# A differential attention layer with its projection slabs woven into the head steps, and a state-space scan that takes its heads in pairs

## What is computed

```python
def diff_pool_layer(x, ...):                       # stage A
    proj = rms_norm(x, norm_g) @ w_in              # 1024 -> q 512, k 512, v 512, u 512
    q, k, v, u = jnp.split(proj, ...)
    q, k = rms_norm per 64-wide half head          # 4 heads, 2 halves each
    a_out = diff_attention(q, k, v, lam, ...)      # softmax(q0 k0) - lam * softmax(q1 k1), times v, causal, ALiBi,
                                                   # then rms_norm over the 128 columns of a head
    b_out = pool_mixer(u, w_group, pool_scale)     # trailing mean minus token, 4 groups of 128, a 128x128 map each
    return x + concat([a_out, b_out]) @ w_out      # 1024 -> 1024

scores = cb[...] * decay                           # scan S: per head and chunk of 128 tokens
y_diag = einsum('bcgels,bcsgep->bclgep', scores, xdt)
y_off  = einsum('bclgn,bcgepn->bclgep', cm, states_in) * exp(a_cs)
```

## Time and profile before

| | |
|---|---|
| median of 3 runs | 2020.97 us (2020.79 to 2022.02) |
| the profiled execution | 2023.49 us, its span 2021.3 us |
| mean granted TensorE clock | 0.984 |
| PE busy | 1944.0 us, 96% of the span |
| DVE, ACT, POOL busy | 1180.1, 795.6, 130.5 us |
| chain that ended last | PE 84%, DVE 9%, ACT 4% |
| moved by DMA | 186.49 MB, mean 92 GB/s |

### The profile page before, as it was taken

How to read it: one execution, slowest core, us unless ns; L and a number is a source line. 1 busy time by engine, 2 the same in 40 slices (tenths; PEclk the granted TensorE clock), 3 DMA queues, 4 the chain that set the end, 5 groups by cost and what they waited for, 6 DMA issues and landing times.

```text
span 2021.3 us, 24744 instructions
## 1 busy us (share of the span) xinstructions
PE 1944.0 (96%) x9034; PEld 1529.7 (76%) x9034; DVE 1180.1 (58%) x1847; ACT 795.6 (39%) x1231; POOL 130.5 (6%) x104
## 2 busy tenths in 40 slices
PE   7967999999999999999999999999999999999999
PEld 6834788888877667888887877777766678888877
DVE  3377566526644765765367487554465657653672
ACT  3144443313433654442234333322356644422341
POOL 2020100000011101000000100111111010000000
PEclk9977999999999999999999999999999999999999
DMA  5200232232222111222221323234342212222213
GB/s 203 94 11 1 83 104 98 79 114 85 79 96 84 63 42 63 85 97 94 99 104 62 115 84 117 99 130 152 120 151 94 79 63 84 98 94 99 104 60 106
DMA packets 38016, 186.49 MB, mean 92 GB/s; under 512 B 4353, under 2 KB 4481, under 8 KB 23089
## 3 DMA queue, kind: packets, MB, share of 16 engines
q1 hardware_dynamic: 37648, 185.22, 26.5%
q10 hardware_dynamic: 288, 0.23, 0.0%
HBM read 176.95 MB, written 8.49 MB: 92 GB/s over the span
## 4 chain that ended last, share of the span: by engine, by line
PE 84%; DVE 9%; ACT 4%; issue 2%; DMA 0%; POOL 0%; SPq 0%; DVEq 0%; ACTq 0%; POOLq 0%
PE banks L676 58%; PE banks L1100 15%; DVE w_lo L1777 1%; DVE tmp L2160 1%; PE banks L1039 1%; PE banks L1017 1%; PE banks L925 1%; PE banks L1026 1%; DVE w_lo L2027 1%; PE banks L1141 1%; PE banks L989 1%; PE banks L1166 1%; ACT w_hi L1265 1%; PE banks L1113 1%; ACT w_hi L1459 1%
## 5 line engine op out<-in xcount | busy, mean ns | idle before, releaser
L676 PE MATMUL banks<-xn_hi,w_hi 128*128 128x512 f32 x1288 | 506.3, 393 | 17.9 <-DVE w_lo L2520 9.6
L676 PE MATMUL banks<-xn_hi,w_lo 128*128 128x512 f32 x1288 | 503.3, 391 | 0.0
L676 PE MATMUL banks<-xn_lo,w_hi 128*128 128x512 f32 x1288 | 498.1, 391 | 0.0
L1777 DVE TENSOR_TENSOR w_lo<-raw,w_hi 128x2048 fp32r<-128x2048 f32 (+2 forms) x139 | 287.2, 2066 | 79.5 <-ACT w_hi L1265 79.4
L1265 ACT ACTIVATE w_hi<-raw 128x2048 fp32r<-128x2048 f32 (+2 forms) x139 | 237.6, 1709 | 225.2 <-PE banks L676 225.2
L676 PEld LDWEIGHTS banks<-xn_hi,w_hi 128*128 128x128 f32 x1288 | 243.2, 189 | 73.0 <-issue 19.9
L676 PEld LDWEIGHTS banks<-xn_lo,w_hi 128*128 128x128 f32 x1288 | 243.1, 189 | 51.7 <-issue 1.0
L676 PEld LDWEIGHTS banks<-xn_hi,w_lo 128*128 128x128 f32 x1288 | 243.3, 189 | 50.8
L1343 ACT ACTIVATE tmp<-scaled_h,par 128x512 f32<-128x512 f32 x132 | 100.6, 809 | 349.7 <-DVE scaled_h L1860 349.7
L676 PE MATMUL banks<-hid_hi,w_hi 128*128 128x512 f32 x528 | 206.4, 391 | 6.9 <-DVE w_lo L1777 5.1
L676 PE MATMUL banks<-hid_lo,w_hi 128*128 128x512 f32 x528 | 205.8, 390 | 0.0
(11 more groups left out here) (258 smaller groups left out, 2387.2 us busy)
## 6 DMA issues: line engine op xcount, KB each, us to landing
raw<-weights SPq DMA_DIRECT2D x116, 1024.0 KB, 4.8
raw<-weights SPq DMA_DIRECT2D x24, 768.0 KB, 4.2
raw<-weights SPq DMA_DIRECT2D x24, 640.0 KB, 3.8
big<-scratch SPq DMA_DIRECT2D x40, 256.0 KB, 4.9
att<-scratch SPq DMA_DIRECT2D x16, 256.0 KB, 4.2
scratch<-stage SPq DMA_DIRECT2D x12, 256.0 KB, 4.2
scratch<-con SPq DMA_DIRECT2D x12, 256.0 KB, 2.2
x<-xt SPq DMA_DIRECT2D x4, 512.0 KB, 8.3
```

Of the source, the lines that this page charges most:

```text
L676: return pe.matmul(psum[:, 2 * p + m, :], w[:, at_:at_ + P], x_part(k), start=start, stop=stop)
L1777: dve.tensor_tensor(w_lo[:, sl], raw[:, sl], w_hi[:, sl].bitcast(F32), ALU.subtract).then_inc(lo_done, 1)
```

## The change

1. Slabs are reordered in stage A: the weights of q, k, v for heads 0 and 1 and of u come first (5 plain slabs, `A_IN`), then q, k, v for heads 2 and 3 (`A_MORE`, 3 slabs), then `A_OUT` in half slabs of 4 input chunks by 4 output chunks, first the two of the pooling half, then the two of the attention half.
2. `A_MORE` and the first two slabs of `A_OUT` are woven into 18 steps g, one for each (head, query block) and two at the end; the other two of `A_OUT` follow. Units use banks 2 and 3.
3. The norms, v transposes, pooling groups and their products, and the norm of each finished head (square, sum, scale, split) are spread over the slabs and the steps. POOL squares q, k and heads 0 to 2 and does three of the splits; it no longer copies v. The pooled chunks get their high part straight from PSUM on ACT, the low part on DVE.
4. The scan does both heads of a pair in one step, with the halves m in turn. `seg` and `c_grow` have 4 buffers each. A chunk of memory, `more` (3 x 512 columns), is added.
5. The first slab of `F0_U0` waits for units only if they used its banks.

```diff
-    ("A_IN", 8, 8, 2), ("A_OUT", 4, 8, 2),
+    ("A_IN", 5, 8, 2), ("A_MORE", 3, 8, 2), ("A_OUT", 4, 4, 4),
-WOVEN = ("C_K", ...)
+WOVEN = ("A_MORE", "A_OUT", "C_K", ...)
+A_FILL = weave([("A_MORE", 3), ("A_OUT", 2)], [20] * 4 + [16] + [12] * 4 + [7] * 8 + [8] + [12, 20])
+        more = at("more", 3 * T)

 PE, stage A
-                    linear("A_IN", xh, xl, (t_hi, xn_ready, 0), 0)
-                    attention("A", A_HEADS, 0, {"v": 0, "t": 0, "o": 0})
...
-                    linear("A_OUT", ...)
+                slab(0, 0, 8, 2, xh, xl, (t_hi, xn_ready, 0))
+                slab(1, 0, 8, 2, xh, xl, between=lambda: stat(0))
+                slab(2, 0, 8, 2, xh, xl, between=lambda: norm_job(0, 4))
+                norm_job(1, 5)
+                slab(3, 0, 8, 2, xh, xl, between=lambda: turn_v(0))
+                slab(4, 0, 8, 2, xh, xl)
+                pe.wait_ge(banks_read, 4)
+                for g in range(A_STEPS + 2):
+                    it = g // 4
+                    if g < A_STEPS:
+                        scores(g)
+                    fill(g)
+                    if 1 <= g <= A_STEPS:
+                        turn(g - 1)
+                    if g % 4 < 2 and it + 1 < A_HEADS:
+                        norm_job(2 * (it + 1) + g % 4, 1)
+                    elif g % 4 >= 2 and it < 2:
+                        pool_product(2 * it + g % 4 - 2)
+                    if g == 1:
+                        turn_v(1)
+                    elif g in (9, 10):
+                        turn_v(g - 7)
+                    elif g % 4 == 3 and it:
+                        squares_summed(it - 1)
+                    if g >= 2:
+                        values(g - 2)
+                fill(A_STEPS + 2)
+                squares_summed(A_HEADS - 1)
+                fill(A_STEPS + 3)
+                for s in (FIRST["A_OUT"] + 2, FIRST["A_OUT"] + 3):
+                    woven(s, 0, 48, a_sub_hi, a_sub_lo, sub_ready)

 DVE, stage A, a step g
+                    if 1 <= g <= A_STEPS:
+                        finish(g - 1)
+                    if g < A_STEPS:
+                        maxima(g)
+                    if g < 2:
+                        pool_group(2 + g)
+                    if g % 4 == 2 and it:
+                        output(it - 1)
+                    if g % 4 in (1, 2) and it + 1 < A_HEADS:
+                        scaled(2 * (it + 1) + g % 4 - 1)
+                    elif g in (3, 4, 7, 8):
+                        pooled_low(2 * ((g - 3) // 4) + (g - 3) % 4)
+                    if g % 4 == 0 and it >= 2:
+                        sub_scale(it - 2, chunk(big, it - 2))
+                    if g:
+                        for s, m in A_FILL[2][g - 1]:
+                            evacuate(s, m)
+                    for q in range(2):
+                        if g >= q + 1:
+                            for s in A_FILL[1][g - q - 1]:
+                                lo_piece(s + 1, q, 2)

 PE, scan (every second head's first step)
-                def head_products(h):
...
+                def pair_products(q):
...
+                    pe.wait_ge(score_ready, 2 * q + 2)
                     for j in range(4):
+                        for m in range(2):
+                            h = 2 * q + m
+                            pe.matmul(psum[64 * m:64 * m + 64, bank, j * P:(j + 1) * P], xdt[:, j, h * 64:h * 64 + 64],
+                                      seg[h % 4][:, j * P:(j + 1) * P], ...)
                     pe.wait_ge(st_taken, 3 * g + 3)
+                    pe.wait_ge(c_ready, 2 * q + 2)
                     for j in range(1, 4):
+                        for m in range(2):
+                            ...  state[j - 1], c_grow[h % 4]

 PE, slab()
-                    if woven_slab(s - 1) or woven_slab(s - 2):
+                    if (woven_slab(s - 1) or woven_slab(s - 2)) and unit_banks(UNITS_BEFORE[s] - 1) == 2 * p:
```

More of the change, by code:

```diff
@@ L220, in blocks_program @@
         bias = [chunk(att, 6), chunk(att, 7)]
[L221 to L227, removed]
+        sq_q, sq_k, sq_o = chunk(tn, 0), chunk(tn, 1), chunk(tn, 2)
+        sub_rs = chunk(more, 0)
         neg_max, row_sum, row_inv = small[:, 0:8], small[:, 8:16], small[:, 16:24]
@@ L325, in blocks_program @@
         acs = [chunk(att, 0), chunk(att, 1)]
-        seg = [chunk(att, 2), chunk(att, 3), chunk(tn, 2)]
+        seg = [chunk(att, 2), chunk(att, 3), chunk(tn, 2), chunk(more, 0)]
         grow = [rs, rsk]
-        c_grow = [chunk(tn, 0), chunk(tn, 1)]
+        c_grow = [chunk(tn, 0), chunk(tn, 1), chunk(more, 1), chunk(more, 2)]
         cs_t = tok[:, 0:192].rearrange("p (j h) -> p j h", j=4)
@@ L440, in body @@
                 def body(i):
-                    if not (a == 0 and isinstance(i, int)):
-                        slab(a, i, k * m * P)
+                    slab(a, i, k * m * P)
                     slab(a + 1, i, k * m * P)
[L444 to L447, removed]
                 if n:
-                    pairs(sp, n, body, head=1 if a == 0 else 0)
+                    pairs(sp, n, body)
                 if (hi - lo) % 2:
@@ L458, in _ @@
                 if step == "A":
-                    stream("A_IN")
-                    stream("A_OUT")
+                    slab(1, 0, slab_columns(1, 0))
+                    sp.dma_start(par[:, GAINS_AT:LATE_AT], params[:, GAINS_AT:LATE_AT]).then_inc(params_in, 16)
+                    late_loads()
+                    for s in range(2, FIRST["F0_U0"]):
+                        slab(s, 0, slab_columns(s, 0))
                 elif step == "C":
@@ L559, in _ @@
                     ffn(step)
-            last = 56
+            last = 48
             for q in range(4):
@@ L569, in _ @@
         def _(pool):
[L570 to L596, removed]
             def sum_squares(base):
@@ L1312, in rms @@
                 act.activation(to, lt[:, :], ACT.Exp, scale=-0.5).then_inc(ready, 1)
-            def high_parts(base, n, dst, c0=0):
-                for c in range(n):
-                    act.wait_ge(t_ready, base + c - DC + 1)
-                    act.activation(chunk(dst, c0 + c), chunk(tn, (base + c) % 3), ACT.Identity).then_inc(t_hi, 1)
             token_norms = [0]
@@ L1572, in decay @@
                     act.wait_ge(seg_ready, 4 * h + 4)
[L1573 removed]
+                    act.activation(seg[h % 4], seg[h % 4], ACT.Exp).then_inc(decay_ready, 1)
                 def square(c):
@@ L2589, in halves @@
     def halves(w):
-        for k in range(0, D, 512):
+        for k in range(0, w.shape[0], 512):
             for n in range(0, D, 512):
@@ L2602, in ffn @@
             c += half
-    linear(a["ab_w_in"][0])
-    linear(a["ab_w_out"][0])
+    for c in (0, 512, 1024, 1536, 1792, 256, 768, 1280):
+        linear(a["ab_w_in"][0], c, c + 256)
+    halves(a["ab_w_out"][0][512:])
+    halves(a["ab_w_out"][0][:512])
     ffn(a["f_w_up"][0], a["f_w_down"][0])
```

858 lines of the change are left out of this document (400 added, 458 removed).

## The result

| | before | changed |
|---|---|---|
| time, median (us) | 2021.27 (4 runs) | 1965.81 (4 runs, 1965.11 to 1966.84) |
| ratio | | 0.9723 [0.971, 0.9736] |
| profiled execution: span (us) | 2021.3 | 1965.1 |
| its mean granted clock | 0.984 | 0.997 |

A forecast was written before the change was run, and what follows sets the result against it. PE, busy 96% of the span, was taken as the bound, with idle time to fill in stage A and only PE's own work to shrink in the scan. 43.3 + 13.3 = 56.6 off 2020.97 gave 1964.4 us, range 1956 to 1976.

The forecast's parts named there:

- stage A: Whole of stage A: F0 starts at 200.4 instead of 243.7, saving 43.3 us.
- The scan: Scan: pairs of 28 records with column halves in turn save 12.4 us, fewer returns 0.9, together 13.3.
- The first five slabs: Start of stage A: five plain slabs with norm sums and v transposes, so the steps begin at 74.8.
- PE's own list: Stage A: PE's work at full clock without waits, 99.7 us for the steps, 21.9 for slabs 10 and 11.
- Wait (a): Stage A, step 2: PE waits 2.1 us for the second half of slab 6's low part from DVE.
- I take 1.00: Stage A's steps: granted clock stays full, since attention X weaves slabs into similar steps at 1.00.
- Wait (b): Stage A, step 15: slab 9 wants a bank that DVE reads behind its maxima, 0.5 us.
- Wait (c): Stage A's tail of half-slab pairs: X's first wait, 1.35 us, comes here too; its second, 1.02, does not.
- Rival 1: Stage A, steps 9 to 16: chain maxima, exponentials, finish sets the step, 36.1 us instead of 31.2; 1969.3 us; chance 0.17.
- Rival 2: Stage A, early steps: DVE-bound, POOL's squares meet low parts four times, 4 us more, 1968.4 us; chance 0.11.
- Rival 3: Scan: the column halves don't overlap, 12.4 us less is saved, 1976.8 us; chance 0.06.
- Rival 5: Stage A's steps: waits bring the clock to 1.2 GHz, up to 2064 us, slower from 57% of steps; chance 0.02.

The follow-up runs named there:

- n4: Changed kernel with DVE adding stage A's last output slab's first unit to x ahead of the low part of F0's first slab: 1964.98 us.
- n9: n8 with DVE's pooled low part ahead of step 7's maxima and slab 9's low pieces moved from steps 10 and 11 to ends of 12 and 13: 1956.88 us.
- n3: Changed kernel with slab 6's second high piece earlier on ACT and both its low pieces at the end of DVE's step 1: 1962.81 us.
- n7: n3 with DVE also reading slab 5's first unit out of its bank at the end of step 1: 1961.13 us.
- n2: Changed kernel with one head's 14 scan records in every second step, buffers and other engines' orders kept: 1981.77 us.
- n6: Changed kernel with 9 instead of 7 woven products in each of steps 9 to 16, and 6 and 10 instead of 12 and 20 behind: 1970.32 us.
- n1: Changed kernel with the pair's heads not in turn in the scan: products grouped by head as 4, 4, 3, 3: 1969.62 us.
- n5: Changed kernel with all seven scan products of a pair's first head, then all seven of the second: 1975.06 us.
- n8: n7 with n4's order of the tail in all three woven stages, A, C and X: 1956.76 us.
- n10: The changed kernel once more, with no edit: 1965.39 us.

## Why the prediction was right, and where it was off

The mechanism of both parts was as forecast. That the total came within 1.4 us (by the profiled spans within 0.4, 1965.1 against 1964.7) is luck in part, because errors had opposite signs: stage A gave 4.0 less than its term, the scan 2.6 more, and 1.0 in the stages between, nearly all of it clock, was in no term. Step by step:

- **The first five slabs**: the steps begin at 74.2, forecast 74.8.
- **PE's own list** (99.7 for the steps, 21.9 for slabs 10 and 11, 121.6): 204.43 - 74.24 = 130.2, less 8.1 of waits and 1.9 lost behind the first of them, is 120.2, where 1.9 holds 1.6 of clock and the 0.3 beyond the wait's length. That is 1.4 less than forecast; 1.0 of it are the 14 fp32 sums, most of which take 0.86 us where woven, not 0.93. The other waits have such extras too (taking away 1.36 in n4 gave 1.7, and 1.09, 0.97 and 0.50 in n9 gave 1.22, 1.19 and 0.72), so PE's own work is some 0.9 us less still.
- **Wait (a)**, slab 6's low part: forecast 2.1, it was 2.98. (The terms in that sum give 92.45 and not 92.6, so 2.0.) Place and cause were right (n3, n7). The step that failed is the sentence on the clock, "I take 1.00": true of 117 of the 130 us, but the clock came down behind the wait and cost 1.6 us more (it came down in six traces of seven that had the wait). X could not show that, since the earlier trace rows hold no wait of this size. The start of stage C in the trace of before could: behind a wait of 2.25 us there, products stand 0.43 apart and the granted clock of 16 us is 0.89.

```profile
622.42 0.47 PE L1100 MATMUL banks<-xn_hi,w_hi 128*128 128x512 f32 x1 [2.25 <-DVE big L2038]
```

- **Wait (b)**: forecast 0.5, it was 0.70. **Wait (c)**: forecast 1.35, it was 1.36, and the one after it stayed away, as forecast from the banks.
- **Waits not on the list**: 1.09 in step 7, 0.97 and 0.50 in steps 11 and 12, 0.49 behind the steps, 3.1 us together. The forecast had added up DVE's load per step and found room. n9 shows that load wasn't the matter: the order was, since a low-part piece (for which DVE itself waited on ACT) or the maxima stood ahead of what PE wanted. In all, 4.1 us of waits more than forecast and 1.9 behind the first of them, 1.4 and 0.6 less of work: the 4.0 that stage A lacks.
- **The scan**: 28 records of a pair took 1.68, forecast 1.79 from X's 16 records (8 x 0.11 = 0.9 us). A return to the fill costs 0.2 us and not 0.11, because the gap ahead of a head is wider too (n2); that and the shorter pair make 8 x 1.91 = 15.3 where 13.3 was forecast. The other 0.6 is a wait of the kernel before that had no term (n2).
- **Rival 1** (steps 9 to 16 bound by the chain) fell: they took 32.7 us with 2.2 of waits in them, 30.5 without, by the list 31.2; n6 lengthened them by the products it added. **Rival 2** fell: no piece of a low part in the early steps was slowed by POOL (1.21 to 1.22 us a piece, for half of what takes 2.29 in the earlier trace rows). What it describes came once and late: slab 10's two pieces took 3.45 us at 170.31 beside POOL. PE's 0.49 us behind the steps come after that on DVE; that they follow from it was not tested. **Rival 3**: n1, n5 and n2 gave back 3.8, 9.3 and 16.0 us; the halves do overlap. **Rival 5**, the slow side, was there in small: 0.87 over 13.4 us, which is some 3.5 us at the low clock and not 57% of the steps.

On rival 3, what X's rows had said holds in the scan as well: all 14 products of a pair use the same 128 rows, and their records run two at a time. The Trainium skill (TensorE: Matmul & The Clock Gate, Part 3: Packing small matmuls) says that a weight load overlaps matmuls in flight only when its row group differs. By that rule n2 and the changed kernel would have differed only by the returns, 1.9 us; they differ by 16.0, so the measurement decides against it here. The same section of the Trainium skill also gives a speedup of 2.38 for three products packed by columns. The prediction left that out, and the runs bear it out in kind: two column halves share the time.

That TensorE lost time on both sides of a head (0.09 and 0.11) agrees with what the Trainium skill says of a change of tiling mode (TensorEngine Tiling, Tiling Modes, Key Properties), that it drains the array; the runs don't separate it from the weights' change.

## What to carry to other kernels

Price a wait on TensorE of some 2 us or more at its length plus what the clock may take behind it (here 1.5 to 2.8 us in six traces, nothing in one), and look for it in the order of the feeding engines' instructions rather than in their load: a sum of busy times per step missed four waits, and moving six instructions of DVE and ACT won back 9 us (n8). Products that fill half of the columns should alternate halves record by record; a block of one half and then the other wins only where the two meet. Where two traces are compared, look for stretches with equal instructions and unequal clock before a gain is booked.

## What the runs showed of the hardware

- Records with the same 128 rows and different column halves run side by side, and the later half's first record starts when three records ahead of it in the program are still to come (n5: 0.54 us saved at one change of half, n1: 1.20 at three). Records of the same half stand 0.11 us apart.
- Behind the 2.98 us wait in step 2 the clock fell from 2.4 to 1.2 GHz in six of the seven traces that had this wait (the changed kernel twice, n1, n2, n4, n6). Step 2 took 11.70 to 11.79 us in five of them and 12.96 in n1, against 10.20 in n5, where the clock stayed: 1.5 to 1.6 us lost, and 2.8 in n1. After 1.12 (n3) it didn't fall. After the same 2.26 us at the start of stage C it fell in some executions and not in others, with the same program (n10).
- A wait cost TensorE 0.1 to 0.3 us more than its listed length (n4, n5, n9).
